# A state-space scan on one core: the input projections of two groups moved ahead by one to two slots

## What is computed

```python
rest = h @ w_in[:, D_INNER:]                 # x (4 x 512), B (4 x 128), C (4 x 128), dt
xbc = silu(_dwconv(rest[..., :CONV_DIM], conv_w, conv_b))   # 5 taps over positions
# per group and direction, chunks of 128:
states = einsum(B, decay_end, x * dt)        # state work
cb = einsum(C, B)                            # one 128x128 matrix per chunk
y_diag = einsum(cb, decay, x * dt)
y_off = einsum(C, prev_state, exp(a_cum))
y = y_f + flip(y_b) + d * x
gy = rms_norm(y * silu(z))                   # z = h @ w_in[:, :D_INNER]
out = gy @ w_out
```

## Time and profile before

| what | value |
|---|---|
| median of 3 runs | 1859.52 us (1858.22 to 1859.78) |
| the profiled execution's own time | 1858.6 us |
| its span in the trace | 1856.3 us |
| granted PE clock, mean over the span | 0.995 |
| first group's scan | 698.4 to 762.1 us |
| second group's scan | 762.1 to 827.2 us |
| third group's scan | 827.2 to 892.3 us |

### The profile page before, as it was taken

How to read it: one execution, slowest core, us unless ns; L and a number is a source line. 1 busy time by engine, 2 the same in 40 slices (tenths; PEclk the granted TensorE clock), 3 DMA queues, 4 the chain that set the end, 5 groups by cost and what they waited for, 6 DMA issues and landing times.

```text
span 1856.3 us, 25612 instructions
## 1 busy us (share of the span) xinstructions
PE 1796.1 (97%) x10135; PEld 1316.2 (71%) x10136; DVE 1131.1 (61%) x1485; ACT 916.9 (49%) x1436; POOL 54.4 (3%) x49
## 2 busy tenths in 40 slices
PE   6989999999999999899999999999999999999997
PEld 5976788888888877687887566666666566655563
DVE  3266466765657797687867565555555555555644
ACT  3335572222246646587756465554454445444443
POOL 1000000000000121100200000000000000000000
PEclk9999999999999999999999999999999999999999
DMA  9456215665455532022259999999999999999995
GB/s 355 147 202 254 91 46 182 201 204 192 151 183 196 160 104 69 27 88 68 92 203 344 393 394 406 409 412 414 409 407 411 412 413 410 408 412 412 413 406 236
DMA packets 182457, 498.21 MB, mean 268 GB/s; under 512 B 10347, under 2 KB 62907, under 8 KB 167995
## 3 DMA queue, kind: packets, MB, share of 16 engines
q1 hardware_dynamic: 181760, 495.93, 70.7%
q10 hardware_dynamic: 571, 0.57, 0.1%
HBM read 495.42 MB, written 1.05 MB: 267 GB/s over the span
## 4 chain that ended last, share of the span: by engine, by line
PE 78%; DVE 8%; ACT 5%; DMA 4%; SPq 3%; issue 2%; ACTq 0%; POOL 0%; DVEq 0%; POOLq 0%
PE bank L974 12%; PE bank L975 11%; PE bank L976 11%; PE bank L1664 9%; PE bank L1656 4%; PE bank L1239 4%; PE bank L1240 4%; PE bank L1241 4%; DMA raw<-in_moe_gu_w_dram 2%; DVE ar L3028 2%; SPq L854 2%; PE bank L1339 1%; PE bank L1340 1%; PE bank L1341 1%; SPq L849 1%
## 5 line engine op out<-in xcount | busy, mean ns | idle before, releaser
L2668 DVE TENSOR_TENSOR lo<-raw,hi 128x1024 fp32r<-128x1024 f32 x182 | 216.6, 1222 | 171.4 <-ACT hi L1958 169.6
L2649 DVE TENSOR_TENSOR lo<-raw,hi 128x1024 fp32r<-128x1024 f32 x172 | 212.0, 1238 | 146.0 <-ACT hi L1938 144.5
L1938 ACT ACTIVATE hi<-raw 128x1024 fp32r<-128x1024 f32 x156 | 164.6, 1059 | 260.0 <-PE bank L1241 172.6
L1958 ACT ACTIVATE hi<-raw 128x1024 fp32r<-128x1024 f32 x182 | 186.4, 1056 | 148.5 <-DMA raw<-in_moe_gu_w_dram 58.2
L974 PE MATMUL bank<-hi,xg_t 128*128 128x512 f32 x448 | 182.4, 407 | 2.5 <-DVE xg_t L3218 1.2
L975 PE MATMUL bank<-lo,xg_t 128*128 128x512 f32 x448 | 175.2, 391 | 0.0
L976 PE MATMUL bank<-hi,xg_t 128*128 128x512 f32 x448 | 174.9, 390 | 0.0
L2668 DVE TENSOR_TENSOR lo<-ar,hi 128x1024 fp32r<-128x1024 f32 x94 | 112.1, 1222 | 90.9 <-ACT hi L1958 89.7
L974 PE MATMUL bank<-hi,hth 128*128 128x512 f32 x400 | 160.0, 400 | 3.0 <-DVE lo L2668 3.0
L975 PE MATMUL bank<-lo,hth 128*128 128x512 f32 x400 | 156.0, 390 | 0.0
L976 PE MATMUL bank<-hi,htl 128*128 128x512 f32 x400 | 155.8, 390 | 0.0
(11 more groups left out here) (400 smaller groups left out, 3288.0 us busy)
## 6 DMA issues: line engine op xcount, KB each, us to landing
raw<-in_moe_gu_w_dram SPq DMA_DIRECT2D x126, 1024.0 KB, 16.5
raw<-in_moe_down_w_dram SPq DMA_DIRECT2D x60, 1024.0 KB, 16.8
ar<-in_moe_gu_w_dram SPq DMA_DIRECT2D x59, 1024.0 KB, 18.2
out_slot<-in_moe_gu_w_dram SPq DMA_DIRECT2D x39, 1024.0 KB, 15.9
ar<-in_moe_down_w_dram SPq DMA_DIRECT2D x33, 1024.0 KB, 15.7
raw<-in_ada_w_dram SPq DMA_DIRECT2D x14, 2048.0 KB, 9.1
raw<-in_ffn_gu_w_dram SPq DMA_DIRECT2D x22, 1024.0 KB, 5.1
raw<-in_ffn_down_w_dram SPq DMA_DIRECT2D x22, 1024.0 KB, 4.9
```

The source lines that it names most:

```text
L1938: A_(hi[:, p % SPL, :], raw[:, slot(u), (p % 2) * PIECE:(p % 2 + 1) * PIECE], ACT.Copy).then_inc(hi_ready, 1)
L1958: A_(hi[:, q % SPL, :], m_raw(i)[:, (q % 2) * PIECE:(q % 2 + 1) * PIECE], ACT.Copy).then_inc(m_hi, 1)
L2649: TT(lo[:, p % SPL, :], raw[:, u, h * PIECE:(h + 1) * PIECE], hi[:, p % SPL, :].bitcast(F32), ALU.subtract).then_inc(done, 1)
L2668: TT(lo[:, q % SPL, :], src[:, (q % 2) * PIECE:(q % 2 + 1) * PIECE], hi[:, q % SPL, :].bitcast(F32), ALU.subtract).then_inc(m_lo, 1)
```

## The change

With `EARLY = 2` the projections of the second and third group (g = 1, 2) are placed anew. Their first x pair moves to slots 8 and 9 of the round before (for g = 1 ahead of the scan, for g = 2 into the first group's scan). The second x pair moves from slots 2 and 3 to slots 1 and 2, B and C from slots 4 and 5 to slots 3 and 4; slots 0 and 5 hold no piece. On ACT `conv_in` of blocks 0 and 1 moves from slot 1 to slot 0; those of blocks 2 and 3 stay in slot 3, those of 4 and 5 in slot 5. On DVE `conv` of blocks 0 and 1 moves from slots 2 and 3 to slots 1 and 2. Five groups of three `fill` are taken out: two ahead of the scan, and one each in slots 7, 8 and 9 of the first group's scan; the group at the start of slot 7 stays. The fourth group is placed as before.

```diff
@@ -636,12 +636,16 @@
 
         SLOTS = 10
 
+        EARLY = 2
+
         def used_by(g, k):
 
+            ahead = max(0, k - 8)
             if g < 0:
-                return 2 * S_GRP + min(k, 6)
-            if g == 0:
-                return 2 * S_GRP + 6 + min(k, 6)
+                return 2 * S_GRP + min(k, 6) + ahead
+            if g < EARLY:
+                a = 2 * S_GRP + (8 if g == 0 else 14 + 10 * (g - 1)) + min(max(0, k - 1), 4)
+                return a + (max(0, k - 6) if g > 0 else 0) + (ahead if g < EARLY - 1 else 0)
             a = 2 * S_GRP + 12 + 10 * (g - 1)
             if g < N_GROUPS - 1:
                 return a + k
@@ -1466,19 +1470,21 @@
                     if k >= 6:
                         ssm_out((k - 6) // 2, (k - 6) % 2)
                     return
-                if k < 4:
-                    proj("x", g, k // 2, k % 2)
+                n = k + 1 if 1 <= g <= EARLY else k
+                if n < 4:
+                    if n >= 2 or not 1 <= g <= EARLY:
+                        proj("x", g, n // 2, n % 2)
+                elif n < 6:
+                    proj("bc", g, 0, n - 4)
                 elif k < 6:
-                    proj("bc", g, 0, k - 4)
+                    pass
                 elif g > 1:
                     proj("z", g - 1, (k - 6) // 2, k % 2)
-                if k == 9 and g == 0:
-                    fill(bank[2][:, 0:256], 3)
+                elif k >= 8:
+                    proj("x", g + 1, 0, k - 8)
                 if k >= 5:
                     to_tok(g, k - 5)
                 if k == 9:
-                    if g == 0:
-                        fill(bank[2][:, 0:256], 3)
                     cb(g)
 
             def late_fill(g, n):
@@ -1498,7 +1504,7 @@
                 if k in (1, 3):
                     state_ctx(g, k // 2)
                 project(g + 1, k)
-                if g == 0 and k >= 7 or g == N_GROUPS - 1 and k in (4, 5):
+                if g == N_GROUPS - 1 and k in (4, 5):
                     late_fill(g, 3)
                 if k >= 2:
                     yy(g, k - 2)
@@ -2293,13 +2299,13 @@
                     if k in (4, 5):
                         norm_hi(k - 4)
                     return
-                for i in {1: (0, 1), 3: (2, 3), 5: (4, 5), 8: (6, 7)}.get(k, ()):
+                if k in (7, 9) and g > 1:
+                    zs(g - 1, (k - 7) // 2)
+                for i in {(0 if 1 <= g <= EARLY else 1): (0, 1), 3: (2, 3), 5: (4, 5), 8: (6, 7)}.get(k, ()):
                     if i >= 2:
                         conv_out(g, i - 2)
                     if i < 6:
                         conv_in(g, i)
-                if k in (7, 9) and g > 1:
-                    zs(g - 1, (k - 7) // 2)
                 if k >= 5:
                     tok(g, k - 5)
                 if k == 9 and g == N_GROUPS - 1:
@@ -3048,8 +3054,9 @@
                     if k in (5, 6):
                         norm_lo(k - 5)
                     return
-                if 2 <= k <= 7:
-                    conv(g, k - 2)
+                at = (1, 2, 4, 5, 6, 7) if 1 <= g <= EARLY else (2, 3, 4, 5, 6, 7)
+                if k in at:
+                    conv(g, at.index(k))
                 if k == 9:
                     dve.wait_ge(cb_t, g + 1)
                     for d in range(2):
```

## The result

The changed kernel takes 1882.9 us in the median (1880.9 to 1885.0, 4 runs), the kernel before in the same session 1858.9 (1857.7 to 1859.8). The ratio is 1.0133 (95% interval 1.0121 to 1.0145): 24 us slower. Forecast were 1877 us and 17 us slower; the range reached to 1884.

A forecast was written before the change was run, and what follows sets the result against it. PE was taken to set slots 0 to 3 before the change, the DVE and ACT chain the rest of a scan. Terms of 6.9, 0.6, 2.0 and 4.3 us gave 13.8, plus 3.5 for the clock: 1877 us, range 1867 to 1884.

The forecast's parts named there:

- the sum: Forecast terms added up: 6.9 + 0.6 + 2.0 + 4.3 = 13.8 us at full clock, +17.3 with the clock's 3.5.
- the list ahead of the scan: PE's to_tok, pieces, cb and four fills from to_tok of block 2 to the first bc, given as 14.8 us.
- the chain in slot 3 of the second scan: From the end of yy to the end of the second conv_in copy, which PE's B and C piece needs: 7.6 us.
- Ahead of the scan: Before the first bc: moved pieces replace only about 4 us of fills and waits, decay chain hidden; +6.9 us.
- First scan, slots 0 to 3: PE waits 2.0 and 5.3 us for conv_in copies, so the work taken out returns as waits; 30.2 us, +0.6.
- First scan, the rest: After slot 3: 20.6 us of DVE and ACT chain, then 15.5 us with the moved pieces; 36.1 us, +2.0.
- Second scan, slots 0 to 3: PE waits 5.5 us in slot 1 and again in slot 3 for conv_in copies; 35.6 us, +4.3.
- Second scan, the rest: After slot 3: keeps its 33.8 us, since the z pieces in slots 6 to 9 are held by the same chain.
- The clock: Half-clock stretches after five PE waits of 4 to 6 us, at most 1.7 each: +3.5 us, bounds 0 to some 10.
- The last rival: Slots 4 to 9: half-speed stretches slow yy, for which seg waits; +3 to +6 us more, 1880 to 1885, chance 0.12.
- The time without the waits: Rival: waits do not come and PE sets slots 0 to 3 of both scans; -4.5 us, 1855, chance 0.07.
- Slots 4 to 9 are set by DVE and ACT: From the yy of slot 3 on, the seg, ce_, m_, conv and mul chain sets the time; 20.6 us to slot 7's yy.

The follow-up runs named there:

- copies_earlier: Changed kernel with ACT's copies out of the banks placed earlier: blocks 0 and 1 ahead of the first ce_ in slot 0, 2 and 3 in slot 2; 1857.9 us (1.0008).
- fills_in_waits: Changed kernel with fills put into PE's waits in slots 1, 3 and 6 of the first two scans; 1875.7 us (1.0104).
- copies_slot4_free_b: Changed kernel with ACT's copies out of the banks earlier, and DVE's conv of block 2 in slot 3 instead of 4; 1858.2 us (0.9997).

## Why the prediction was right

The sign, the places and the mechanism were right: the copies out of the bank came late, and copies_earlier shows that they were the cause. The time was in the upper end of the range, because the clock and one wait were priced too low. At full clock the sum was 13.8 us; 16 are found (6.4, 3.4 and 6.2 in A, B and C, with the steps of fills_in_waits where it has full clock), and 9.1 for the clock instead of 3.5. The terms of the sum have two slips of 0.1 us: the list ahead of the scan adds up to 14.9, and the chain in slot 3 of the second scan to 7.7. Step by step:

- *Ahead of the scan*: forecast +6.9, found +6.4, with no wait in it. The decay chain was hidden, as bounded.
- *First scan, slots 0 to 3*: the waits were forecast as 2.0 and 5.3 and came as 2.08 and 5.35. The walk took 35.1 us instead of the 30.2 of the sum; the two pieces behind the waits took 7.2 and 7.1 from start to start instead of 5.5 and 4.3, which is the clock.
- *First scan, the rest*: forecast 36.1, found 36.4, with the `yy` of slot 7 at 20.7 us (forecast 20.6).
- *Second scan, slots 0 to 3*: forecast 35.6, found 40.3. The wait of slot 3 was right (5.62 for 5.5), that of slot 1 was 6.81 instead of 5.5, and the two pieces again ran at half clock for a part, at a cost of 1.6 and 1.4. The 1.3 us of the wait go with something that the sum left out. PE's state matmuls now stand right behind `bc`, so POOL's next two products start 1.7 us into the scan, beside DVE's `gated` and the added low part. These two took 1.99 and 2.06 us here, and 1.23 and 1.21 before. POOL's timeline of the changed kernel:

```profile
775.46 1.04 POOL L950 TENSOR_TENSOR ar<-ar 128x512 f32<-128x512 f32 x1 [6.45 <-PE bank L1407]
776.47 2.02 POOL L950 TENSOR_TENSOR raw<-ar 128x512 f32<-128x512 f32 x1
```

And DVE's, of the same time:

```profile
775.60 1.99 DVE L3118 TENSOR_TENSOR ar<-ar,raw 128x1024 f32<-128x1024 f32 x1
777.51 2.06 DVE L2655 TENSOR_TENSOR lo<-raw,hi 128x1024 fp32r<-128x1024 f32 x1
```

The Trainium skill ("GPSIMD Engine Reference", Specifications) says that GpSimd shares its SBUF interfaces with VectorE, with contention from DVE instructions that have two inputs in SBUF. Both DVE instructions here have two. The trace agrees for POOL's second product, which took 2.02 us, and for both of DVE's; the first product took 1.04 us beside the same work. No run took this overlap away by itself, so that it made the wait longer is argued, not shown.

- *Second scan, the rest*: forecast 33.8, found 35.7; the z piece behind the wait of slot 6 took 5.3 us instead of 2.9, and began 14.4 us behind the `yy` of slot 3, as before.
- *The clock*: this is the term that was mis-sized. Forecast were 3.5 us, "a little under half the price of the five"; by the steps above it is 9.1, near the upper bound of some 10. Five waits of 3.8 to 6.8 us were followed by slow stretches, as forecast, but four of these lasted 6.8 us instead of 3.4, and a sixth, of 3.4 us, came after the wait of only 2.08. A part of each was to lie in the wait; it was 8.5 of the 34.1 us together, the largest part in slot 1 of the second scan (3.5 of 6.8). The stretch in slots 6 and 7 of the first scan cost nothing (36.4 for 36.1).
- *The last rival* (a longer chain in slots 4 to 9, 1880 to 1885) has the measured time in its range, but not its mechanism: the `yy` of slot 7 of the first scan and the z piece of slot 6 of the second came where the chain of before puts them.
- *The time without the waits* was given as 4.5 us under the kernel before, plus the clock. The run with the copies earlier came at 0.5 above, with 17 us at half clock and the new wait of 2.3; this agrees only with those two added; no run has the repair without them.
- *Slots 4 to 9 are set by DVE and ACT*: true for what was forecast, but narrower than I read it. When a conv is taken out, PE's `yy` takes over after 0.8 us.

## What to carry to other kernels

When work is moved ahead on one engine of a hand-written schedule, the work that frees its output buffer must move ahead too: here all but a quarter of the loss came from copies that stood too late in another engine's queue, behind a chain that begins at the moved engine itself, and from the clock behind the waits for them. The length of that chain can be read from the trace of before, where the work now gone had hidden it. Price each new PE wait with the clock, here from 2.08 us on: the long piece behind it ran in part at half speed and took 1.4 to 2.8 us more, while half speed in short work that ends in a wait cost nothing.

## What the runs showed of the hardware that was not expected

A wait of 5.35 us on PE was followed by a stretch of 6.8 us at half clock, twice the one before the change, although matmuls ran without a pause from 729.26 on; a wait of 5.62 us by one of 3.4. The same wait of 2.34 us at `state_lat` was followed by a stretch at half clock in five profiles and by none in a sixth (copies_slot4_free_b). Half clock over 17.1 us of A to C instead of 3.4 left the time of the kernel before as it was (1858.1 against 1857.8 us), but only since the fills that were taken out gave back what it cost. And DVE's product of 128x1024 took 1.99 us beside POOL's, 1.23 alone.
